# Row tiles 2 and 3 of x: split in natural layout and turned by DMA instead of by TensorE

## The reference

```python
h = rmsnorm(x, norm_pre_g)                 # rows normalized over 1024 columns
u = h @ w_in                               # 512 x 1024 times 1024 x 4096
dq, dk, dv, dg, mq, mk, mv, mg = split(u, 8 groups of 512 columns)
a = diff_attention(dq, dk, dv, lambda, subln_g, bias)   # 4 heads, two softmax maps each
b = moba_attention(mq, mk, mv, bias)                    # 8 heads, blocks of 256 keys
y = concat(a * silu(dg), b * silu(mg)) @ w_out          # 512 x 1024 times 1024 x 1024
x = x + rmsnorm(y, norm_post_g)
```

## Time and profile before

| what | value |
|---|---|
| median of 3 runs | 261.27 us (260.73 to 262.19) |
| the profiled execution's own time | 263.27 us |
| its span | 261.5 us |
| PE busy | 249.4 us (95%) |
| DVE busy | 177.5 us (68%) |
| ACT busy | 143.5 us (55%) |
| POOL busy | 30.4 us (12%) |
| mean granted TensorE clock | 0.996 of full speed |

### The profile page before, as it was taken

The page is one execution under the profiler, slowest core; times in us unless marked ns, Lnnn a source line. Parts: engine busy times, 40 slices in busy tenths (PEclk is TensorE's granted clock), DMA queues, the critical chain, the costliest instruction groups (busy, mean ns, idle before and its releaser), DMA issues.

```text
span 261.5 us, 4394 instructions
## 1 busy us (share of the span) xinstructions
PE 249.4 (95%) x1581; PEld 123.3 (47%) x1581; DVE 177.5 (68%) x383; ACT 143.5 (55%) x335; POOL 30.4 (12%) x76
## 2 busy tenths in 40 slices
PE   7689999999999999999999989999999999999990
PEld 7445444444444544544455434444544444554440
DVE  2587785338849688798678576875698786934223
ACT  3784973236546475685475685665645675721111
POOL 2059000000000050050004014000000000110101
PEclk9999999999999999999999999999999999999998
DMA  6994697297415343753422864576907739999404
GB/s 220 385 311 116 193 345 235 82 345 237 116 36 131 93 112 100 197 128 102 120 84 61 176 139 147 125 193 153 168 13 143 140 60 173 220 194 261 120 3 162
DMA packets 55402, 41.42 MB, mean 158 GB/s; under 512 B 41536, under 2 KB 41800, under 8 KB 55380
## 3 DMA queue, kind: packets, MB, share of 16 engines
q1 hardware_dynamic: 55380, 41.14, 59.5%
HBM read 29.04 MB, written 2.13 MB: 119 GB/s over the span
## 4 chain that ended last, share of the span: by engine, by line
PE 82%; DVE 6%; ACT 5%; DMA 3%; issue 2%; POOL 1%; SPq 0%; DVEq 0%; POOLq 0%; ACTq 0%
PE unit_ps L510 71%; PE score_ps L529 5%; PE o_ps L549 5%; DMA stage<-in_w_in_dram 3%; DVE w_lo L732 2%; ACT arena L649 1%; DVE w_lo L730 1%; ACT junk L595 1%; ACT w_hi L609 1%; DVE v_lo L773 1%; PE score_ps L471 1%; ACT area L641 1%; ACT w_hi L608 1%; DVE arena L822 0%; DVE area L788 0%
## 5 line engine op out<-in xcount | busy, mean ns | idle before, releaser
L510 PE MATMUL unit_ps<-w_hi,area 128*128 128x512 f16 x256 | 80.7, 379 | 3.6 <-DVE area L788 2.3
L510 PE MATMUL unit_ps<-area,w_hi 128*128 128x512 f16 x256 | 76.2, 379 | 0.0
L649 ACT ACTIVATE arena<-arena,negmax 128x512 f32<-128x512 f32 (+3 forms) x64 | 35.4, 554 | 48.4 <-DVE negmax L802 48.1
L510 PE MATMUL unit_ps<-area,w_lo 128*128 128x512 f16 x128 | 48.5, 379 | 0.0
L510 PE MATMUL unit_ps<-w_lo,area 128*128 128x512 f16 x128 | 48.5, 379 | 0.0
L510 PEld LDWEIGHTS unit_ps<-w_hi,area 128*128 128x128 f16 x256 | 25.0, 98 | 34.1 <-DVE area L788 2.7
L510 PEld LDWEIGHTS unit_ps<-area,w_hi 128*128 128x128 f16 x256 | 23.8, 98 | 26.5 <-issue 0.8
L802 DVE CUSTOM_DVE_ANT_0 arena<-score_ps,strips 128x512 f32<-128x512 f32 (+3 forms) x64 | 28.6, 484 | 8.6 <-PE score_ps L529 8.6
L730 DVE SCALAR_TENSOR_TENSOR w_lo<-stage,g_cols,w_hi 128x512 f16<-128x512 f32 x32 | 24.1, 754 | 11.4 <-ACT w_hi L609 11.3
L608 ACT ACTIVATE w_hi<-stage,g_cols 128x512 f16<-128x512 f32 x32 | 22.7, 710 | 5.1 <-DMA stage<-in_w_in_dram 5.1
L732 DVE SCALAR_TENSOR_TENSOR w_lo<-stage,g_cols,w_hi 128x512 f16<-128x512 f32 x32 | 24.8, 776 | 0.0
(11 more groups left out here) (78 smaller groups left out, 314.7 us busy)
## 6 DMA issues: line engine op xcount, KB each, us to landing
stage<-in_w_in_dram SPq DMA_DIRECT2D x32, 512.0 KB, 4.4
stage<-in_w_out_dram SPq DMA_DIRECT2D x8, 512.0 KB, 3.8
arena<-in_x_dram SPq DMA_DIRECT2D x4, 512.0 KB, 9.7
strips<-bias_rows SPq DMA_DIRECT2D x1, 2048.0 KB, 8.9
stage<-in_x_dram SPq DMA_DIRECT2D x4, 512.0 KB, 4.4
out_dram<-area SPq DMA_DIRECT2D x3, 512.0 KB, 2.7
strips<-bias_rows SPq DMA_DIRECT2D x1, 1024.0 KB, 5.7
g_row<-in_norm_post_g_dram SPq DMA_DIRECT2D x1, 512.0 KB, 10.3
```

The lines of the kernel that those rows point to most:

```text
L510: last = nc.tensor.matmul(bank, a, b, start=(k == 0 and n == 0), stop=(k == KT - 1 and n == 2))
L649: nc.scalar.activation(probs[:, i % 2, m, 0:n], probs[:, i % 2, m, 0:n], ACT.Exp, bias=negmax[:, i, m:m + 1], scale=-1.0, accum_out=sums[: ...
```

## The change

For row tiles 2 and 3 the normalized x is split before it is turned. ACT writes the hi half of the whole tile from `x_sb` with the scale `x_rstd` (`xn_hi`), DVE writes the lo half from `x_sb`, `x_rstd` and that hi half (`xn_lo`), both into `x_halves`, a view of the buffer `pt` that the attention uses later. SyncE then turns each half by a DMA transpose into `ht` (`turn_x`): the turns of tile 2 stand between the loads of quarters 5 and 6, those of tile 3 between the loads of quarters 7 and 8. The transposes on PE, `x_norm`, `x_hi` and `x_lo` of the two tiles are gone. On ACT `xn_hi(2)` stands ahead of `x_square(3)`, and `xn_hi(3)` behind the reading of unit 0. On DVE `xn_lo(2)` stands behind `x_lo(1)`, and `xn_lo(3)` behind the reading of unit 0. Units 2 and 3 run as `turned_unit`: 8 matmuls hi by hi, 8 hi by `w_lo`, and last 8 with the lower half of x.

```diff
--- before.py
+++ after.py
@@ -188,6 +188,7 @@
         gates = sb("gates", [P, 2, TILES, WIDTH])
         strips = sb("strips", [P, HEADS, SEQ])
         pt = sb("pt", [P, 2, 4 * TILES, P], fp16)
+        x_halves = pt[:, :, :, :].rearrange("p b (h k) s -> p b h (k s)", h=2)
         g_row = sb("g_row", [P, DM])
         g_rows = g_row[0:KT, 0:P]
         g_cols = sb("g_cols", [P, KT])
@@ -262,6 +263,9 @@
         xs_ready = sem("xs_ready")
         ht_hi_ready = sem("ht_hi_ready")
         ht_ready = sem("ht_ready")
+        xn_hi_ready = sem("xn_hi_ready")
+        xn_lo_ready = sem("xn_lo_ready")
+        x_turned = [[sem(f"x_turned{t}_{h}") for h in range(2)] for t in range(2, TILES)]
 
         unit_done = sem("unit_done")
         unit_read = sem("unit_read")
@@ -343,6 +347,11 @@
                 sp.wait_ge(y_ready, t + 1)
                 sp.dma_start(out_v[t], y_sb[:, t % 2, :]).then_inc(stored[t % 2], 16)
 
+            def turn_x(t, h):
+                sp.wait_ge(xn_lo_ready if h else xn_hi_ready, t - 1)
+                sp.dma_start_transpose(ht[:, h, :, t * P:(t + 1) * P], x_halves[:, t - 2, h, :])\
+                    .then_inc(x_turned[t - 2][h], 16)
+
             def load_x(t):
                 sp.dma_start(x_sb[:, t, :], x_v[t]).then_inc(x_loaded[t], 16)
 
@@ -359,8 +368,15 @@
                 sp.dma_start(rel_t, rel_bias.rearrange("b h -> h b")).then_inc(rel_loaded, 16)
             sp.dma_start(lam_in[:, :, :], diff_lambda[0].partition_broadcast(P)).then_inc(small_loaded, 16)
             sp.dma_start(subln[:, :], diff_subln_g[0].partition_broadcast(P)).then_inc(small_loaded, 16)
-            for n in range(4, 9):
-                load_quarter(n)
+            load_quarter(4)
+            load_quarter(5)
+            for h in range(2):
+                turn_x(2, h)
+            load_quarter(6)
+            load_quarter(7)
+            for h in range(2):
+                turn_x(3, h)
+            load_quarter(8)
             sp.wait_ge(row_built, 1)
             sp.dma_start(bias_rows.ap(), row_sb).then_inc(rows_stored, 16)
             sp.wait_ge(rows_stored, 16)
@@ -464,8 +480,6 @@
         def _(pe):
             def x_transposes(t, part=0):
                 pe.wait_ge(xs_ready, x_count(t, part))
-                if t >= 2:
-                    pe.wait_ge(ht_ready, x_count(t - 2, X_PARTS[t - 2] - 1))
                 n = KT // X_PARTS[t]
                 for k in range(part * n, (part + 1) * n):
                     last = nc.tensor.transpose(score_ps[:, 2 * (t % 2) + k // 4, (k % 4) * P:(k % 4 + 1) * P],
@@ -487,7 +501,10 @@
                     elif u >= 2:
                         pe.wait_ge(unit_freed, u - 1)
                     if kind != "y":
-                        pe.wait_ge(ht_ready, x_count(i if kind in "vg" else TILES - 1))
+                        need = i if kind in "vg" else TILES - 1
+                        pe.wait_ge(ht_ready, x_count(min(need, 1)))
+                        for t in range(2, need + 1):
+                            pe.wait_ge(x_turned[t - 2][1], 16)
                 if kind == "y" and q % 2 == 0:
                     pe.wait_ge(a_turned[q // 2], 16 * (i + 1))
                 if (u, q) == (0, 2):
@@ -512,6 +529,21 @@
                 if q == 3:
                     last.then_inc(unit_done, 1)
 
+            def turned_unit(u):
+
+                _, half, i, g = unit_of(u)
+                bank = unit_ps[:, u % 2, :]
+                rows = slice(i * P, (i + 1) * P)
+                pe.wait_ge(unit_freed, u - 1)
+                pe.wait_ge(split_lo, 4 * (g + 1))
+                for h, b in ((0, w_hi), (0, w_lo), (1, w_hi)):
+                    if b is w_hi:
+                        pe.wait_ge(x_turned[i - 2][h], 16)
+                    for k in range(KT):
+                        last = nc.tensor.matmul(bank, ht[:, h, k, rows], b[:, g % 3, k, :],
+                                                start=(k == 0 and h == 0 and b is w_hi), stop=(k == KT - 1 and h == 1))
+                last.then_inc(unit_done, 1)
+
             def scores(i):
 
 
@@ -558,13 +590,17 @@
             for part in range(X_PARTS[0]):
                 x_transposes(0, part)
             warm_up(WARM_UP[2])
-            for u in range(FIRST_UNITS):
+            for q in range(4):
+                unit_quarter(0, q)
+                if q == 1:
+                    x_transposes(1)
+            for q in range(4):
+                unit_quarter(1, q)
+            turned_unit(2)
+            turned_unit(3)
+            for u in range(TILES, FIRST_UNITS):
                 for q in range(4):
                     unit_quarter(u, q)
-                    if (u, q) == (0, 1):
-                        x_transposes(1)
-                if u + 2 < TILES:
-                    x_transposes(u + 2)
             for j in range(SLOTS):
                 if j == 0:
                     for u, q in FILL[0][0]:
@@ -671,6 +707,11 @@
                 nc.scalar.activation(a_halves[half][:, 0:WIDTH], gates[:, half, t, :], ACT.Copy,
                                      scale=1.0 / GATE_SCALE).then_inc(a_hi_ready, 1)
 
+            def xn_hi(t):
+                act.wait_ge(x_rstd_ready, t + 1)
+                nc.scalar.activation(x_halves[:, t - 2, 0, :], x_sb[:, t, :], ACT.Copy,
+                                     scale=x_rstd[:, t:t + 1]).then_inc(xn_hi_ready, 1)
+
             def x_square(t):
                 act.wait_ge(x_loaded[t], 16)
 
@@ -686,10 +727,11 @@
             split(3)
             x_square(2)
             x_hi(1)
+            xn_hi(2)
             x_square(3)
             for u in range(FIRST_UNITS):
-                if u + 2 < TILES:
-                    x_hi(u + 2)
+                if u == 1:
+                    xn_hi(3)
                 for n in SPLIT_AT_UNIT[u]:
                     split(n)
                 unit(u)
@@ -782,6 +824,12 @@
                 nc.vector.tensor_scalar(x_sb[:, t, cols], x_sb[:, t, cols], x_rstd[:, t:t + 1], 1.0,
                                         ALU.mult, ALU.mult).then_inc(xs_ready, 1)
 
+            def xn_lo(t):
+                dve.wait_ge(xn_hi_ready, t - 1)
+                nc.vector.scalar_tensor_tensor(x_halves[:, t - 2, 1, :], x_sb[:, t, :], x_rstd[:, t:t + 1],
+                                               x_halves[:, t - 2, 0, :], ALU.mult, ALU.subtract)\
+                    .then_inc(xn_lo_ready, 1)
+
             def x_lo(t, part=0):
                 dve.wait_ge(ht_hi_ready, x_count(t, part))
                 dst, src = x_part(t, part)
@@ -889,9 +937,8 @@
             x_norm(1)
             split(2)
             split(3)
-            x_norm(2)
             x_lo(1)
-            x_norm(3)
+            xn_lo(2)
 
             dve.wait_ge(small_loaded, 32)
             dve.wait_ge(x_half_squared, 1)
@@ -901,8 +948,8 @@
                                                op0=ALU.mult, op1=ALU.add,
                                                accum_out=lam_dot[:, i:i + 1]).then_inc(lam_dots, 1)
             for u in range(FIRST_UNITS):
-                if u + 2 < TILES:
-                    x_lo(u + 2)
+                if u == 1:
+                    xn_lo(3)
                 for n in SPLIT_AT_UNIT[u]:
                     split(n)
                 unit(u)
```

## The result

The changed kernel takes 265.75 us (median of 6 executions, 264.92 to 266.78) against 261.51 us (6 executions) for the kernel before, measured beside it on the same chip: a ratio of 1.0168, 95% interval 1.0144 to 1.0192. It is slower by 4.24 us. The direction is the one forecast and the time lies in the range (260.4 to 266.6), but the loss is nearly twice the 2.3 us of the sum. Two executions further down, one of four in experiment 8 and one of eleven in experiment 11, ran over 1.5% above the fastest of their kernel and are left out of its median.

The account below looks back on a forecast made before the run. PE was taken to bound the kernel, with a second chain from POOL to DVE 2.7 us behind; PE's 2.5 us gain is lost waiting at unit 5, 2.3 us on top: 261.27 + 2.3 = 263.6 us, range 260.4 to 266.6.

Parts of the forecast that it names:

- the sum: Whole kernel: PE's early gain of 2.5 us gone and 2.3 us on top, 261.27 + 2.3 = 263.6 us.
- PE's gain: Units 1 to 3 on PE: without the transposes and waits around them, unit 3 starts 2.5 us earlier.
- The turns' landing: DMA turns of x ahead of unit 2: each lands in 3.0 to 5.6 us, 3.7 in the middle.
- the destination's stride: DMA turns: stride differs from line 339, unpriced by any row, between nothing and twice the landing; taken as nothing.
- The bias row's two steps: POOL's copies start 1.7 to 1.9 us later, then DVE blocks them: they end at 31.0 against 25.75.
- SyncE's queue: Turns of tile 2 hold the queue until about 22.0; quarter 8 goes out at 26.2, costing nothing.
- rival 2: POOL is not shut out by DVE: unit 5 starts 0.8 us earlier than before, 260.4 us; chance 0.16.
- Strips to unit 5: Strips issued at 33.0, quarter 9 split 7.0 us later, unit 3 read and unit 5 started at 44.8.
- a wait of 4.9 us: PE, done with unit 4 at 39.9, waits 4.9 us for unit 5, which starts at 44.8.
- taking the clock to stay up: Forecast without a fall of PE's clock in the wait ahead of unit 5: 263.6 us; chance 0.45.
- rival 1: Clock falls in the wait ahead of unit 5: 1.7 to 5.2 us more, most likely about 266; chance 0.28.

Follow-up runs that it names:

- experiment 8: Changed kernel with `x_square(3)` put ahead of `xn_hi(2)` on ACT: 266.24 us, ratio 1.0137 against the kernel before.
- experiment 11: Changed kernel with loads of quarters 9 to 11 ahead of the bias row wait and quarter 8 ahead of tile 3's turns: 260.82 us, ratio 0.9967.
- Experiment 7: Changed kernel with POOL's 32 bias row copies written as memsets of 0: 265.93 us in one execution.
- experiment 4: Changed kernel with 24 small identity matmuls, read by nobody, on PE ahead of unit 5: 265.42 us, ratio 1.0147.
- experiment 6: Changed kernel run again with no edit: 265.34 us, ratio 1.0160 against the kernel before.
- experiment 5: Changed kernel with 11 small matmuls on PE ahead of unit 5: 263.62 us, ratio 1.0090.
- experiment 1: Kernel before, run and profiled again with no edit: 260.59 us.
- experiment 2: Changed kernel with loads of quarters 9, 10 and 11 ahead of SyncE's wait for the bias row: 260.78 us, ratio 0.9969.
- experiment 12: Changed kernel with tile 3's turns alternating with loads of quarters 6 to 8, and quarters 9 to 11 ahead of the bias row: 260.71 us, ratio 0.9986.
- experiment 9: Changed kernel with only the load of quarter 8 moved ahead of tile 3's two turns on SyncE: 263.69 us, ratio 1.0097.
- experiment 10: Changed kernel with quarter 8 loaded ahead of tile 3's turns and POOL's copies written as memsets of 0: 264.02 us, ratio 1.0123.

## Why the prediction was right or wrong

**PE's gain: right.** Unit 2 starts 7.76 us behind the anchor, the forecast said 7.8. The turns' landing was near the mark (3.2 to 6.3 us against 3.0 to 5.6), and costing the destination's stride at nothing held: with a quiet queue a turn lands in 3.2 to 3.4 us, where the earlier trace rows has 3.0 at the least.

**The bias row's two steps: right in mechanism, 0.9 us too late.** `x_square(3)` starts at 17.93 behind `xn_hi(2)`, and the copies 4.9 us behind the anchor as forecast. They end 0.9 us earlier than forecast, because six of them, and not eight or more, take 0.7 us or longer: the last get through before DVE reaches the split of quarter 7 (28.78), which the forecast had them meet. A copy that meets `xn_lo(3)` is blocked for the whole of it; in the profile of after, POOL's copies from 21.8 to 22.3 us, and DVE beside them:

```profile
L442 POOL COPY gates<-gates x5: 173/173/1262, 21.8 to 22.3; 12x1 f32<-12x1 f32 x5
```
```profile
22.25 1.28 DVE L829 SCALAR_TENSOR_TENSOR pt<-arena,x_rstd,pt 128x1024 f16<-128x1024 f32 x1
```

One copy takes 1262 ns where the others take 173, as long as the DVE instruction with its two SBUF inputs (1.28 us). Experiment 7's memsets ran in 1.50 us together beside the split of quarter 4 (20.40 to 21.81), which held two of the changed kernel's copies for 0.72 and 0.74 us; `xn_lo(3)` came behind them. The Trainium skill, page "SBUF — State Buffer", section "Who interferes with whom", has this rule (GpSimd's reads contend, its writes alone do not), and both traces agree.

**SyncE's queue: wrong, and hidden.** I priced the turns' issue at about 1.4 us each and had quarter 8 go out at 26.2 (24.8 shifted); it went out at 27.24, as the second turn of tile 3 took 3.64 us of issue. The forecast had the store free of quarter 8 and gave the step from the copies to the strips 2.0 us; with quarter 8 issued 1.5 us ahead of the store it took 2.65. That, and 0.5 us more from the strips to quarter 9, used up the 0.9 us that the copies were early: that unit 5 came out within 0.2 us of the forecast is in part luck. The queue also made rival 2's number wrong: it needs both chains early, and the 0.16 that I gave it was for one.

**Strips to unit 5: right, within 0.5 us.** 7.5 us from the strips' issue to the split of quarter 9 (forecast 7.0), 4.8 from there to the start of unit 5 (forecast 4.8). Unit 5 is 2.5 us later than before, forecast 2.3. The wait was 3.6 us and not 4.9, since 1.1 of it was paid ahead of units 3 and 4; that moves nothing.

**The step that failed: taking the clock to stay up.** The sum had no term for the clock. The prediction had read in the earlier trace rows that the clock falls behind PE's last matmul, and it forecast a wait of 4.9 us. (It read 3.8 us; a mean of 0.85 over 259.0 to 259.5 puts the fall at 259.35, 4.0 us behind 255.35.) By these rows a fall in such a wait was the likelier case, yet it got a chance of 0.28 against 0.45, on the ground that PE nowhere restarts after such a fall; that ground says that the price is unseen, not that the fall is unlikely. The distance is no fixed one, either. At the end of the program, where PE has no more work, the fourteen profiles have the fall between 2.0 and 5.1 us behind its last matmul, in eleven of them under 4.9. The shortest is experiment 4 (last matmul to 257.58), the longest experiment 6 (to 257.32), in windows as above:

```profile
259.50:260.00 0.50, 0.00 (x0) 0.00 (x0) 0.50 (x1) 0.00 (x0) 0.00 (x0) 0.60 0.52 205
```
```profile
262.00:262.50 0.50, 0.00 (x0) 0.00 (x0) 0.00 (x0) 0.00 (x0) 0.00 (x0) 0.96 0.23 82
```

The wait that came, 3.64 us, was shorter than the 4.0 of the prediction's rows, and the clock fell all the same, 3.85 us behind the last matmul, when PE had just restarted. The price was bounded well: "a third to all of its 5.2 us", at least 1.7. It was a third, eight matmuls of 24, and 1.69 us by experiment 5. With this term the forecast would have been 261.27 + 2.3 + 1.7 = 265.3 us, and rival 1's "about 266" is close to what was measured.

**What the sum is now.** From the anchor to the end the changed kernel takes 250.1 us against 246.5, in two profiles each: 3.5 us more. Unit 5 gives 2.5 and the clock 1.7. Against them stand 0.35 at the very end and 0.4 in the attention loop (199.6 us from the first scores to the end of the last matmul in experiment 1's profile, 199.2 in that of after; 0.1 of it are PE's waits for turned probabilities). The 0.35 is one line of the chain, ahead of DVE's last instruction. In experiment 1's profile, and in that of after:

```profile
254.43 0.41 issue
```
```profile
259.39 0.06 issue
```

**What stays open.** Why that issue is shorter, and where the other 0.3 us of the loop went. Why the medians differ by 4.0 to 4.2 us where the profiles differ by 3.5, and why experiments 2, 11 and 12 show 0.6 to 0.9 us in their medians where their profiles have 1.2 to 1.7 from the anchor: the start scatters by 2.5 us, and no run isolates it. Why the second turn of tile 3 holds the queue for 3.6 us: it does so directly behind the first turn and with loads in flight, not in experiment 12, nor for tile 2, where the turns are as close (1.3 us each) but no load is in flight. The times point at the first turn's landing; no run shows the cause.

## What to carry to other kernels

A gain on the bounding engine is worth no more than the slack of the next chain, and a DMA that is put into an in-order queue moves all that stands behind it: read what the queue issues next, and who waits for that. When a forecast contains a wait of TensorE, look up how far behind PE's last matmul this kernel's traces show the clock falling, and take that as a spread (here 2.0 to 5.1 us) and not as a limit; a wait that reaches into the spread gets the half-speed stretch as a term of the sum (of the waits here, those of 3.5 us and more had the fall four times in four, those of 2.6 us not in two). When two producers feed one DMA, making one earlier shows little; shorten both, or take what depends on it (here the next loads) out from behind it.

## What the runs showed of the hardware that I had not expected

- A DMA transpose of 128 x 1024 float16 costs SyncE 1.24 to 1.35 us of issue in most of these kernels (up to 2.1 in experiments 9 to 11), but two back to back behind the loads of two or three quarters 4.9 to 6.2 us together, the issue of the second ending 1.1 to 1.2 us before the first lands. One lands in 3.2 to 3.6 us with a quiet queue, and in 5.4 to 7.3 behind the loads of two or three quarters.
- PE idle for 2.6 us (experiments 9 and 10) left the clock at its upper level, and idle for 3.5 to 3.7 us (the changed kernel twice, experiments 7 and 8) it fell each time, 3.4 to 4.5 us after the last matmul had ended, so in three of the four when PE had already restarted; it was low for 3.4 us each time. At the end of the program it fell 2.0 to 5.1 us after the last matmul in the fourteen profiles. 11 small matmuls, 2.6 us, in the wait kept it up.
- The start of the same program, from its first instruction to its first split, differed by 2.5 us between two executions (5.88 and 8.38 us), which is as much as PE's whole early gain from this change.
